# Output projections of sixteen feed-forward groups as seven block products, with the residual kept in DRAM meanwhile

## The reference, cut to what matters

```python
def swiglu(x, w_in, w_out):
    gate, up = jnp.split(x @ w_in, 2, axis=-1)
    return (jax.nn.silu(gate) * up) @ w_out
...
h = h + mix
h = h + swiglu(rmsnorm(h, norm_ffn[layer]), w_ffn_in[layer], w_ffn_out[layer])
```

## Time and profile before

| | |
|---|---|
| time, median of 3 runs (lowest to highest) | 2312.67 us (2311.14 to 2313.27) |
| the profiled execution: its time / span of its trace | 2311.9 / 2310.1 us |
| busy: TensorE / VectorE / ScalarE / GpSimd | 98% / 68% / 43% / 6% |
| granted clock of TensorE, mean | 0.998 of full speed |
| first feed-forward layer / second, from its first to its last matmul | 331 to 1005 us / 1626 us to the end |

### The profile page before, as it was taken

How to read it: one execution, slowest core, us unless ns; L and a number is a source line. 1 busy time by engine, 2 the same in 40 slices (tenths; PEclk the granted TensorE clock), 3 DMA queues, 4 the chain that set the end, 5 groups by cost and what they waited for, 6 DMA issues and landing times.

```text
span 2310.1 us, 29500 instructions
## 1 busy us (share of the span) xinstructions
PE 2266.7 (98%) x10729; PEld 1873.8 (81%) x10729; DVE 1570.8 (68%) x1907; ACT 986.5 (43%) x1499; POOL 130.9 (6%) x83
## 2 busy tenths in 40 slices
PE   8999999999999999999999999989999999999998
PEld 7788877888888888878888888877888888888886
DVE  7667788666666666687666666665776666666665
ACT  5553465323332232256666665653532333223324
POOL 4000000000000000020111111102100000000000
PEclk9999999999999999999999999999999999999999
DMA  5121201111111111131111101032111111111112
GB/s 147 46 64 53 56 19 40 52 55 55 51 43 52 54 55 55 36 120 28 29 38 37 36 28 37 28 100 60 51 55 55 55 49 44 53 54 54 55 55 82
DMA packets 167318, 123.47 MB, mean 53 GB/s; under 512 B 5081, under 2 KB 148673, under 8 KB 167233
## 3 DMA queue, kind: packets, MB, share of 16 engines
q1 hardware_dynamic: 165504, 118.04, 17.2%
q10 hardware_dynamic: 1728, 4.31, 0.7%
HBM read 113.89 MB, written 8.45 MB: 53 GB/s over the span
## 4 chain that ended last, share of the span: by engine, by line
PE 89%; DVE 7%; ACT 2%; issue 1%; DMA 0%; ACTq 0%; POOL 0%; DVEq 0%
PE ps L1098 36%; PE ps L930 29%; PE ps L1262 11%; PE ps L1309 3%; PE ps L1296 3%; PE ps L1396 2%; PE ps L1277 2%; PE ps L1274 1%; DVE rxl L2002 1%; DVE resid L2022 1%; PE ps L1375 0%; DVE sq_ffn L2410 0%; PE ps L1235 0%; DVE xl L2006 0%; PE ps L1276 0%
## 5 line engine op out<-in xcount | busy, mean ns | idle before, releaser
L2022 DVE TENSOR_TENSOR resid<-ps,resid 128x1024 f32<-128x1024 f32 x204 | 249.2, 1223 | 156.1 <-PE ps L930 150.8
L1623 ACT ACTIVATE ring_h<-raw_ffn 128x512 fp32r<-128x512 f32 x304 | 187.9, 627 | 349.3 <-PE ps L930 200.5
L2261 DVE TENSOR_TENSOR ring_l<-raw_ffn,ring_h 128x512 fp32r<-128x512 f32 x304 | 210.6, 699 | 174.6 <-ACT ring_h L1623 173.7
L930 PE MATMUL ps<-hh,ring_h 128*128 128x512 f32 x672 | 207.5, 390 | 3.0 <-DVE resid L2022 1.6
L930 PE MATMUL ps<-hl,ring_h 128*128 128x512 f32 x672 | 206.9, 389 | 0.0
L930 PE MATMUL ps<-hh,ring_l 128*128 128x512 f32 x672 | 206.9, 389 | 0.0
L930 PEld LDWEIGHTS ps<-hh,ring_h 128*128 128x128 f32 x672 | 126.3, 188 | 30.0 <-DVE resid L2022 2.0
L1262 PE MATMUL ps<-xh,wh_att 128*128 128x512 f32 x368 | 149.6, 406 | 0.0
L1623 ACT ACTIVATE ring_h<-w_sum 128x512 fp32r<-128x512 f32 x80 | 48.0, 625 | 236.4 <-PE ps L930 194.5
L930 PEld LDWEIGHTS ps<-hl,ring_h 128*128 128x128 f32 x672 | 126.3, 188 | 26.3
L930 PEld LDWEIGHTS ps<-hh,ring_l 128*128 128x128 f32 x672 | 126.1, 188 | 26.2
(11 more groups left out here) (357 smaller groups left out, 5461.3 us busy)
## 6 DMA issues: line engine op xcount, KB each, us to landing
raw_ffn<-in_w_ffn_in SPq DMA_DIRECT2D x88, 512.0 KB, 5.0
raw_ffn<-in_w_ffn_out SPq DMA_DIRECT2D x44, 512.0 KB, 4.2
raw<-in_w_rec_in SPq DMA_DIRECT2D x16, 512.0 KB, 5.6
raw_att<-in_w_kvf SPq DMA_DIRECT2D x16, 512.0 KB, 4.0
xin<-in_x SPq DMA_DIRECT2D x4, 1024.0 KB, 9.6
raw<-in_w_rec_out SPq DMA_DIRECT2D x8, 512.0 KB, 3.9
raw_att<-in_w_q SPq DMA_DIRECT2D x8, 512.0 KB, 3.7
spill<-resid SPq DMA_DIRECT2D x8, 512.0 KB, 3.9
```

The costliest lines, as they stand in the source:

```text
L930: last = pe.matmul(acc[:, h], w, v[:, h], start=(first and p == 0), stop=(final and p == 2))
L1623: act.activation(F.ring_h[slot][:, :], src, ACT.Copy).then_inc(F.unit_hi, 1)
L2022: dve.tensor_tensor(resid[:, m, :], ps[slot][:, :], resid[:, m, :], ALU.add).then_inc(drained[slot], 1)
L2261: dve.tensor_tensor(F.ring_l[slot][:, :], src, F.ring_h[slot][:, :].bitcast(F32), ALU.subtract).then_inc(F.unit_lo, 1)
```

## The change

The output projection of hidden groups 1 to 8, executed in groups 2 to 9 of the loop, becomes a block product too: the 256 hidden features of a group are two tiles of 128, the tokens two halves, the output features two halves of four tiles of 128 (n = 0 to 3). Seven products of 4 tiles x 3 matmuls take the place of the 96 matmuls (`out_products`). The hidden activations need sums of blocks for it (`h_sum`, T1 to T4) and their high and low parts (`h_part_high`, `h_part_low`); the output weights need sums as well (`weight_sum` with "O"), and seven units instead of four. ScalarE copies four sets of four tiles out of PSUM (`out_tap`: s1, u2, s5, c21), VectorE joins three sets of four (`out_join`: C11, C22, C12).

The 16 result tiles of a group (128 x 512, C11, C12, C21 and C22 for each n) are not added to `resid` by VectorE. GpSimd issues a DMA for each that adds it to the DRAM tensor `spill` (`add_outputs`, with `accum_op`). The residual goes to `spill` when group 1 has added its output (8 DMAs by GpSimd) and comes back in the last group (8 DMAs by SP, ahead of the loads of that group); in between, the SBUF space of `resid` holds the result tiles and two of the four split sums. The projections of hidden groups 0, 9 and 10 stay as they were. The loops take four groups a turn, and gate values use one buffer for both sets (`gate_of`).

The core of the diff; left out are renamed counters, the semaphores, the buffers' declarations and the ends of the functions shown:

```diff
@@ TensorE
+            def out_products(F, g):
+                for i in (P1, P2, P6, P5, P7, P3, P4):
+                    slot, count = unit(g, PRODUCTS + i)
+                    part = PART[i]
+                    pe.wait_ge(F.unit_lo, count)
+                    pe.wait_ge(h_part_lo, out_at(F, g, 6, {"B11": 1, "T1": 2, "B21": 3, "B22": 3, "T2": 4, "T3": 5, "T4": 6}[part]))
+                    for n in range(4):
+                        w, y = out_banks(n)
+                        if i == P2 and n in (0, 3):
+                            pe.wait_ge(F.joined, joined_at(g, 2 if n == 0 else 3))
+                        elif i in (P6, P7, P3):
+                            pe.wait_ge(out_tapped, out_at(F, g, 16, {P6: 0, P7: 4, P3: 8}[i] + n + 1))
+                        elif i in (P5, P4):
+                            pe.wait_ge(out_joined, out_at(F, g, 12, (0 if i == P5 else 4) + n + 1))
+                        acc = y if i in (P2, P5, P3) else w
...
 def pair_products (set 1 of these groups; likewise ahead of P2 and P6)
+                if behind:
+                    pe.wait_ge(out_joined, out_at(F, g, 12, 9))
                 product(F, w, unit(g, off), PART[P1], True, True, lows)
@@ ScalarE
 def tap
-                act.wait_ge(hl_ready if what == "s5" else h_ready, times(g, 2, 2 * F.f * GROUPS + j - 1))
+                    act.wait_ge(h_ready, times(g, 2, 2 * F.f * GROUPS + j - (g == 1 and j == 0)))
+            def out_tap(F, g, what):
+                for n in range(4):
+                    w, y = out_banks(n)
+                    i, at = {"s1": (P1, 0), "u2": (P6, 4), "s5": (P5, 8), "c21": (P4, 12)}[what]
+                    act.wait_ge(out_product, out_at(F, g, 28, 4 * i + n + 1))
+                    if what == "s1":
+                        act.wait_ge(added[n], added_at(F, g))
+                    elif what == "c21":
+                        act.wait_ge(c11_added[n], out_at(F, g, 16, 16))
+                    dst = out_part[n][{"s1": 0, "u2": 1, "s5": 2, "c21": 0}[what]]
+                    act.activation(dst[:, :], y if what == "s5" else w, ACT.Copy).then_inc(out_tapped, 1)
@@ VectorE, group
+                    h_sum(F, g, "T4")
+                    h_part_low(F, g, "T3")
+                    weight_sum(F, g, "O", 1, 2)
+                    join(F, g, 0, "C22")
...
+                    pair_low(F, g, "O", P7)
+                    out_join(F, g, "C11")
+                    pair_low(F, g, "O", P3)
+                    weight_sum(F, g, 1, 1, 2)
+                    h_sum(F, g, "T1")
+                    pair_low(F, g, "O", P4)
+                    weight_sum(F, g, 1, 3)
+                    out_join(F, g, "C22")
+                    pair_low(F, g, 1, P1)
+                    out_join(F, g, "C12")
@@ GpSimd
+            def add_outputs(F, g):
+                def add(n, block, m, half):
+                    sem = c11_added[n] if (m, half) == (n, 0) else added[n]
+                    pool.dma_start(spill[m, :, half * BANK:(half + 1) * BANK], block[:, :],
+                                   accum_op=ALU.add).then_inc(sem, 16)
...
+            def all_outputs(F):
+                for m in range(KT):
+                    slot, n = out_tile(F, 1, m)
+                    pool.wait_ge(drained[slot], n)
+                    pool.dma_start(spill[m], resid[:, m, :]).then_inc(added[m % 4], 16)
+                for g in range(2, LAST):
+                    add_outputs(F, g)
@@ SP, load_groups, last group
+                sp.wait_ge(out_product, out_at(F, LAST, 28, 0))
+                for n in range(4):
+                    sp.wait_ge(added[n], added_at(F, LAST))
+                    sp.wait_ge(c11_added[n], out_at(F, LAST, 16, 0))
+                for m in range(KT):
+                    sp.dma_start(resid[:, m, :], spill[m]).then_inc(reloaded[m], 16)
+                load_rest(F, LAST)
```

More of the change, by code:

```diff
@@ L201, in sem @@
             return life.enter_context(nc.semaphore(name))
-        resid = sb("resid", [P, KT, S], F32)
+        with ExitStack() as whole:
+            resid = sb("resid", [P, KT, S], F32, whole)
+        out_part = [[sb(f"c11_{n}", [P, BANK], F32), sb(f"c12_{n}", [P, BANK], F32)] for n in range(4)]
+        out_t = []
+        for n in range(4):
+            out_part[n].append(sb(f"c22_{n}", [P, BANK], F32))
+            out_t.append(sb(["t3h_out", "t3l_out", "t4h_out", "t4l_out"][n], [P, BANK], F32R))
         rstd = sb("rstd", [P, S], F32)
@@ L1116, in pair_products @@
                 w, x, y = banks(j)
-                off = SECOND_UNIT * j
+                off = set_unit(g, j)
                 lows = F.part_lows if isinstance(g, int) and g == 1 and j == 0 else None
+                behind = j == 1 and not is_plain(g)
                 if lows is not None:
@@ L1166, in ffn0 @@
                 group(F0, 1)
-                group(F0, 2)
-                with pe.Fori(1, (GROUPS - 1) // 2) as it:
-                    for d in range(2):
+                with pe.Fori(0, (LAST - 2) // UNROLL) as it:
+                    for d in range(UNROLL):
                         group(F0, (it, d))
+                group(F0, LAST)
                 def part(m, k):
@@ L1729, in rec_to_ffn, with group @@
                     part_high(F, "T4", k)
-            def group(F, g, last=False):
-                prev = before_group(g)
-                if isinstance(g, int) and g == 1:
+            def group(F, g):
+                prev, last = before_group(g), g == LAST
+                if g == 1:
                     tap(F, g, 0, "u2")
@@ L1780, in groups @@
                 group(F, 1)
-                group(F, 2)
-                with act.Fori(1, (GROUPS - 3) // 2) as it:
-                    for d in range(2):
+                with act.Fori(0, (LAST - 2) // UNROLL) as it:
+                    for d in range(UNROLL):
                         group(F, (it, d))
-                group(F, GROUPS - 2)
-                group(F, GROUPS - 1, True)
+                group(F, LAST)
                 pair_silu(F, GROUPS - 1, 1)
@@ new lines, in out_join @@
+            def out_join(F, g, what):
+                for n in range(4):
+                    w, y = out_banks(n)
+                    i, tap, block = {"C11": (P2, 0, 0), "C22": (P7, 8, 2), "C12": (P3, 4, 1)}[what]
+                    dve.wait_ge(out_product, out_at(F, g, 28, 4 * i + n + 1))
+                    dve.wait_ge(out_tapped, out_at(F, g, 16, tap + n + 1))
+                    c = out_part[n][block][:, :]
+                    dve.tensor_tensor(c, w if what == "C22" else y, c, ALU.add).then_inc(out_joined, 1)
@@ L2517, in group @@
+                if last:
+                    hidden_low(F, g, 0)
+                else:
+                    h_part_low(F, g, "B11")
+                    h_part_low(F, g, "T1")
                 pair_low(F, g, 1, P7)
```

471 lines of the change are left out of this document (334 added, 137 removed).

## The result

The changed kernel takes 2295.61 us (median of 6 runs, 2292.78 to 2299.75) against 2311.81 us before: ratio 0.9928, 95% interval 0.9918 to 0.9939. It is 16.2 us faster, where about 41 were forecast. The profiled execution took 2297.0 us, its span 2295.1.

The account below looks back on a forecast made before the run. TensorE was taken to bound the kernel: 2311.9 us less 43.5 for 192 fewer matmuls, plus 2 for the reload, is 2270.4; the runs' median lies 0.8 above, so 2271 us. The range reached from 2265 to 2297.

Parts of the forecast that it names:

- The price of a matmul: TensorE: 0.2267 us each; 192 fewer in the output projections save 43.5 us, a group becomes 57.1 us.
- VectorE's load: Looped group: 28 operations of 512 columns gained, 9 of 1024 lost, +8.3 us, making 48 of 57.1 us.
- three slacks: Looped group: copy s1 of set 0 has 0.65 us, join C22 about 1.7, the output's joins C11 1.2.
- the joins C11: Output on VectorE: last bank joined at 529.3, wanted by product P5 at 530.4; slack given as 1.2 us.
- I take 1.2 ... Sixteen are 19 us of 57: GpSimd's issue of each adding DMA, taken between 0.43 and 2.0 us; sixteen in each group.
- about 30: Last group: the reload waits for the last add, about 30 us after the start of group 9's output.
- It just fits ... I take 1 us in each layer: Last group: output weights queued behind the reload land near 48 us, ScalarE wants them at 49.7; cost 1 us a layer.
- about 8 us late: Last group: lateness of the output weights behind the reload if each add's issue takes 2.0 us.
- some 10 us: Reload's delay in each layer if each GpSimd issue costs 2.4 us.
- GpSimd starved: Rival: each add's issue waits out a VectorE operation; about 2304 us; chance 0.20 together with small stalls.
- Small stalls: Rival: GpSimd's adds slow VectorE, 0.5 to 1.5 us a group, 2278 to 2295; chance 0.20 together with starvation.
- Late adds: Rival: C11 adds landing late hold up copies c21, then TensorE at P6; 2480 us at twice the landing; chance 0.14.

Follow-up runs that it names:

- plain writes: The changed kernel with GpSimd's adding DMAs made plain writes of the same tiles, leaving out the sum into DRAM: 2273.16 us, ratio 0.9831.
- both edits: The changed kernel with the last group's output weights loaded ahead of the reload and all eight looped groups in one turn: 2272.47 us, ratio 0.9828.
- sixteen rows: The changed kernel with each adding DMA cut to 16 of 128 partitions, the rest of the sum left out: 2274.05 us, ratio 0.9837.

## Why the prediction was wrong

**What held.** The price of a matmul and the pace: 57.33 us for a group against 57.1, 0.22 x 16 = 3.5 us less gain. VectorE's load was 45.85 us (forecast 46 to 48): its operations of 512 columns start 0.60 us apart when nothing holds them (875.35, 875.95), and the 0.69 that the prediction summed overlap, as it had said of the matmuls' 0.39. ScalarE's was 30.2 (31.5). None of the three slacks gave out in the loop, and VectorE held up nothing. The copies c21 didn't wait: the fourth C11 add was issued by 876.3 and its buffer wanted at 884.5, and the four copies ran one behind another, in no group with a DMA as what ended a wait:

```profile
882.44 2.62 ACT L1863 ACTIVATE c<-ps 128x512 f32<-128x512 f32 x4
```

One of the slacks was counted too wide: from 517.82 two operations of 1024 and ten of 512 columns end at 527.2 by the prediction's own prices, not 526.5, which leaves 0.5 us and not 1.2 at the joins C11.

**The step that failed: the adds were priced by their issue.** "I take 1.2 ... Sixteen are 19 us of 57" counted GpSimd's time for each and one landing at the end. An issue cost less than that, 0.87 us; what wasn't counted is that each add holds the DMA engines for 1.72 us, in a group whose weights need them too. The last add landed 41.6 us after the output's start (906.63 - 865.04), where "about 30" stood; with plain writes it was 27.9, near the forecast. So the reload and what queues behind it came 11.6 us late, and "It just fits ... I take 1 us in each layer" became 7.4 and 7.9. The prediction had the place and the queue, but not the reason, so it took the near end. That its far end reads "about 8 us late", close to what came, is luck: sixteen issues of 2.0 us in place of 1.2 are 12.8 us more, and 48 + 12.8 is 11 us behind 49.7. In the same way the "some 10 us" of *GpSimd starved* would be 17.5 by its own 2.4 us. Moving the output weights ahead of the reload showed it: 14.7 of the 15.3 us came back.

**The term that was missing: the jump back.** The prediction had no sentence on it. Four groups a turn instead of two cost 7.2 us: the body's instructions are loaded again in each turn (the record of instruction loads; that the two-group body stays loaded is read from their absence before), and at the jump the engines stand while loads and adds share the DMA engines. Without the jump the loss is gone, though instructions are still loaded among adds; with plain writes 0.66 and 0.78 us are left; adds beside the two-group body cost nothing. That the engines wait for just these loads is inferred: the profile names no releaser for their waits.

43.5 - 3.5 - 15.3 - 7.2 = 17.5 us; the two spans differ by 15.0, the medians by 16.2. Of the 2.5 us between 17.5 and 15.0, 1.66 lie ahead of the first feed-forward product, which starts at 332.60 against 330.94; this differs by execution (331.15 with all eight groups in one turn, 332.86 with both edits). The other 0.8 wasn't followed.

**The rivals.** *Small stalls* came nearest in time (2278 to 2295) but not in the cause: VectorE's subtraction for a unit took 687 ns before and after (420 to 950 us). The 1558 ns of the earlier trace rows is a mean: half of the 31 passes took 1.22 us or less, the longest 2.81. It stands beside GpSimd's elementwise work and said nothing of its DMA issues. *GpSimd starved*: its gaps were there, 233 us of them, but shrank with the bytes while VectorE's load stayed. The Trainium skill's rule (SBUF — State Buffer, section SBUF: two separate sides) would make GpSimd wait to write descriptors while VectorE runs an operation in a fast mode. No run here shows it: VectorE's operations keep the paces of the earlier trace rows, an issue lasted 0.87 us as an add and 0.54 as a plain write beside the same load, and the DMA engines were full in the gap. *Late adds* is real but needed four more adds a group; its price at 6.5 us late was 65.00 - 57.33 = 7.7 in that group. The formula of the Trainium skill (DMA: Bandwidth & Descriptors, section Anatomy of one DMA) gives 2.6 us for 256 KB, an estimate from that page. From issue to landing the fastest plain write took 2.3 us, near it, the fastest add 3.6 and the median one 6.0, so it doesn't carry over to adds in a busy queue.

## What to carry to other kernels

A DMA is priced three times: by the engine that issues it, by its landing, and by how long it keeps the DMA engines; here the burst ended when the third sum said so, and what queued behind "all have landed" moved with it. Where a reload must wait for such a burst, put the loads that are needed sooner ahead of it on the queue; here that alone gave 14.7 us, and with the loop's jump removed as well the kernel takes 2272.5 us, 4.2 above what the count of matmuls promised (2311.8 - 43.5 = 2268.3). When a loop's body grows, look at the record of instruction loads at the jump, above all where the DMA engines are busy.

## What the hardware showed that was not expected

- An adding DMA of 256 KB from SBUF to DRAM took 64 packets more than a plain write of the same tile (39168 and 22784 in the queue, over 256 tiles), about 1.72 us of all 16 DMA engines in place of 0.69 (estimates from the queue's share of the time), and 0.87 us of GpSimd in place of 0.54.
- GpSimd issued three adds at the start of a burst and then stood between the later ones, 233 us in 162 waits; with plain writes it was 55.7 us, with sixteen rows 2.0. That it waits for room is inferred.
- TensorE, VectorE and ScalarE stood 2.5, 3.5 and 5.0 us at a jump back to a body that is loaded again, with the DMA engines full of adds; the group lost 3.3 us, 0.7 with plain writes.
